# Triple mixers of a two-block kernel: the output product by blocks of columns, with its own buffer for the mix

## The reference

```python
    for l in range(DEPTH):
        x = x + 0.5 * swiglu_2(rms_norm_2(x, ffn1_norm[l]), ffn1_w1[l], ffn1_w3[l], ffn1_w2[l])
        h = rms_norm_2(x, mix_norm[l])
        z = h @ w_in[l]
        ...
        gt = jax.nn.sigmoid(gates.reshape(B, S, N_BRANCH, D))
        mixed = (gt[:, :, 0] * (y_na @ w_br_na[l])
                 + gt[:, :, 1] * (y_gla @ w_br_gla[l])
                 + gt[:, :, 2] * (y_mla @ w_br_mla[l]))
        x = x + mixed @ w_out[l]
        x = x + 0.5 * swiglu_2(rms_norm_2(x, ffn2_norm[l]), ffn2_w1[l], ffn2_w3[l], ffn2_w2[l])
```

## Time and profile before

| | us |
|---|---|
| median of three runs | 2333.51 |
| lowest and highest | 2332.92, 2333.69 |
| the profiled execution | 2333.37 |
| its span | 2331.5 |
| PE busy | 2320.1 |
| DVE busy | 1682.0 |
| ACT busy | 1257.6 |

### The profile page before, as it was taken

One profiled execution on the slowest core, in us unless ns is written; L12 is line 12 of the kernel. 1 busy time (PEld: TensorE's weight loads), 2 busy tenths in 40 slices (PEclk: granted clock), 3 DMA queues, 4 the chain that ended last, 5 costly groups with the idle time before them and its releaser, 6 DMA issues.

```text
span 2331.5 us, 32711 instructions
## 1 busy us (share of the span) xinstructions
PE 2320.1 (100%) x13658; PEld 2026.8 (87%) x13658; DVE 1682.0 (72%) x2148; ACT 1257.6 (54%) x1525; POOL 74.4 (3%) x106
## 2 busy tenths in 40 slices
PE   9999999999999999999999999999999999999999
PEld 8889889888888978888888877888888888788887
DVE  8867846875876789767766766587587667766873
ACT  6545664554554665545545754555455457554552
POOL 2000000000000010100010000001000100000000
PEclk9999999999999999999999999999999999999999
DMA  7655445565655426656655533567565555344664
GB/s 226 196 185 176 145 134 191 183 192 185 196 184 186 153 91 192 207 190 190 195 187 181 176 129 129 167 195 216 185 193 186 184 182 179 118 136 163 192 187 144
DMA packets 335042, 409.51 MB, mean 176 GB/s; under 512 B 7894, under 2 KB 285104, under 8 KB 334896
## 3 DMA queue, kind: packets, MB, share of 16 engines
q1 hardware_dynamic: 331632, 401.66, 53.9%
q0 software_dynamic: 3072, 5.69, 1.0%
q10 hardware_dynamic: 192, 0.08, 0.0%
HBM read 406.35 MB, written 1.05 MB: 175 GB/s over the span
## 4 chain that ended last, share of the span: by engine, by line
PE 93%; DVE 5%; ACT 1%; DMA 1%; issue 0%; SPq 0%; DVEq 0%; ACTq 0%
PE bank L613 13%; PE acc L613 12%; PE bank L1381 11%; PE bank L621 7%; PE acc L621 6%; PE acc L705 6%; PE bank L705 6%; PE acc L692 4%; PE bank L712 3%; PE acc L712 3%; PE acc L789 3%; PE acc L2762 2%; PE acc L1551 2%; DVE part_lo L503 1%; PE bank L651 1%; PE bank L3334 1%
## 5 line engine op out<-in xcount | busy, mean ns | idle before, releaser
L503 DVE TENSOR_TENSOR part_lo<-raw,part_hi 128x2048 fp32r<-128x2048 f32 (+3 forms) x390 | 870.0, 2234 | 345.9 <-ACT part_hi L496 342.7
L496 ACT ACTIVATE part_hi<-raw 128x2048 fp32r<-128x2048 f32 (+3 forms) x390 | 728.4, 1868 | 335.6 <-DMA raw<-in_ffn_w 99.3
L613 PE MATMUL bank<-hT,part_hi 128*128 128x512 f32 x1408 | 328.2, 390 | 0.3 <-ACT part_hi L496 0.3
L613 PEld LDWEIGHTS bank<-hT,part_hi 128*128 128x128 f32 x1408 | 261.7, 188 | 53.2 <-ACT part_hi L496 0.5
L613 PE MATMUL acc<-hT,part_hi 128*128 128x512 f32 x1280 | 298.2, 390 | 0.0
L613 PEld LDWEIGHTS acc<-hT,part_hi 128*128 128x128 f32 x1280 | 237.8, 188 | 47.6
L1381 PE MATMUL bank<-part_hi,hT 128*128 128x512 f32 x768 | 247.4, 395 | 0.7 <-issue 0.7
L621 PE MATMUL bank<-hT,part_lo 128*128 128x256 f32 x1408 | 184.3, 284 | 0.0
L621 PEld LDWEIGHTS bank<-hT,part_lo 128*128 128x128 f32 x1408 | 178.1, 191 | 3.6
L1381 PEld LDWEIGHTS bank<-part_hi,hT 128*128 128x128 f32 x768 | 144.2, 188 | 32.8 <-issue 3.5
L621 PE MATMUL acc<-hT,part_lo 128*128 128x256 f32 x1280 | 166.4, 283 | 0.2 <-DVE part_lo L503 0.2
(11 more groups left out here) (536 smaller groups left out, 3291.5 us busy)
## 6 DMA issues: line engine op xcount, KB each, us to landing
raw<-in_ffn_w SPq DMA_DIRECT2D x122, 1024.0 KB, 5.3
raw<-in_w_in SPq DMA_DIRECT2D x48, 1024.0 KB, 5.1
raw<-in_ffn_w_up SPq DMA_DIRECT2D x44, 1024.0 KB, 5.4
raw<-in_ffn_w_gate SPq DMA_DIRECT2D x43, 1024.0 KB, 5.4
raw<-in_ffn_w_down SPq DMA_DIRECT2D x32, 1024.0 KB, 5.1
raw<-in_hy_w_in SPq DMA_DIRECT2D x22, 1024.0 KB, 5.0
raw<-in_ffn_w_down SPq DMA_DIRECT2D x16, 768.0 KB, 4.3
raw<-in_ffn_w SPq DMA_DIRECT2D x12, 768.0 KB, 4.6
```

What stands on the lines that cost most here:

```text
L496: t.e.activation(part_hi[:, n % SLOTS, 0:size], raw[:, n % SLOTS, 0:size], ACT.Copy).then_inc(hi_ready, 1)
L503: t.e.tensor_tensor(part_lo[:, n % SLOTS, 0:size], raw[:, n % SLOTS, 0:size], part_hi[:, n % SLOTS, 0:size].bitcast(F32), ALU.subtract).th ...
L613: mm = pe.matmul(tiles[:, f, :].rearrange("p (h s) -> p h s", h=2), slot_cols(s, 0)[:, k, f * P:(f + 1) * P], hT[:, :, k, :], start=(first ...
```

## The change

- `mixT` is a buffer of its own for the turned mix, high and low part side by side. Before, the mix lay in `hT`, where the next activations go.
- `w_out` comes as O0: rows 0 to 511 of columns 256 to 767; O1: all rows of columns 0 to 255; O2: rows 512 to 1023 of columns 256 to 767; O3: all rows of columns 768 to 1023. So output tiles 0 and 1 (pair 0) are finished with O1, tiles 2 and 3 in the middle of O2, 4 and 5 with O2, 6 and 7 with O3.
- Each output tile has a whole bank, its low products in the second half: 16 matmuls per piece of 512 columns (`wide`) and 16 of 256 (`narrow`), 128 a layer.
- `mix_out_scalar` and `mix_out_vector` take the place of `down_scalar`, `down_vector`, `pre_scalar` and `pre_vector` here: copy, add, high parts, low parts and squares pair by pair, with the splits of U0 and G1 between them.
- The banks of the turning always start with bank 0.

The diff, without lines of context:

```diff
@@ -332,6 +332,8 @@
+            with ExitStack() as g:
+                mixT = sb("mixT", [P, 2, KD, S], F32R, where=g)
@@ -2716,8 +2719,11 @@
             load_gates(2)
             for r in (0, 2):
                 load_rows(t, A["w_br_mla_2"][l], r)
-            for r in range(0, 8, 2):
-                load_rows(t, A["w_out_2"][l], r)
+            w = A["w_out_2"][l]
+            load(t, cols_of(w, COLS, WIDE)[:, 0:4, :])
+            load_cols(t, w, 0)
+            load(t, cols_of(w, COLS, WIDE)[:, 4:8, :])
+            load_cols(t, w, COLS + WIDE)
 
         def later_loaded(l):
 
@@ -3410,38 +3416,82 @@
-            def out_tile(s, d, k, passes=PASSES):
-                return down_tile(pe, lambda w: slot_rows(s, w)[:, k % 2, :], lambda g: hT[:, g, k, :], d, k == 0,
-                                 k == KD - 1, passes)
+            def out_bank(d):
+                return bank[:, d, :] if d < 2 else acc[:, d - 2, :] if d < 6 else bank[:, d - 4, :]
+            def wide(d, weights, ks, first=False, last=False):
+                for k in ks:
+                    mm = pe.matmul(out_bank(d).rearrange("p (h s) -> p h s", h=2), weights(0, d, k), mixT[:, :, k, :],
+                                   start=(first and k == ks[0]), stop=(last and k == ks[-1]), skip_group_check=True)
+                return mm
+            def narrow(d, weights, ks, first=False, last=False):
+                for k in ks:
+                    mm = pe.matmul(out_bank(d)[:, 0:S], weights(1, d, k), mixT[:, 0, k, :],
+                                   start=(first and k == ks[0]), stop=(last and k == ks[-1]), skip_group_check=True)
+                return mm
+            def half_rows(s, k0):
+                return lambda part, d, k: slot_part(s, part, 4, WIDE)[:, k - k0, (d - 2) * P:(d - 1) * P]
+            def all_rows(s, d0):
+                return lambda part, d, k: slot_cols(s, part)[:, k, (d - d0) * P:(d - d0 + 1) * P]
+            turned = t.banks.next
+            t.banks.skip(-turned % 4)
-            s = arrived(t)
+            w = half_rows(arrived(t), 0)
-            pe.wait_ge(mix_hi, 4 * l + 1)
-            for d in range(4):
-                for k in (0, 1):
-                    out_tile(s, d, k, ((0, 0), (0, 1)))
-            pe.wait_ge(*banks[0])
-            for d in range(4):
-                for k in (0, 1):
-                    out_tile(s, d, k, ((1, 0),))
+            for i in range(2):
+                pe.wait_ge(mix_hi, 4 * l + i + 1)
+                for d in (2, 3):
+                    narrow(d, w, (2 * i, 2 * i + 1), first=(i == 0))
+            for i in range(2):
+                pe.wait_ge(*banks[i])
+                for d in (2, 3):
+                    wide(d, w, (2 * i, 2 * i + 1))
-            for d in range(4, KD):
-                for k in (0, 1):
-                    mm = out_tile(s, d, k)
+            for d in (4, 5):
+                wide(d, w, range(0, 4), first=True)
+            for d in (4, 5):
+                mm = narrow(d, w, range(0, 4))
-            for k0 in range(2, KD, 2):
-                s = arrived(t)
-                for d in range(KD):
-                    for k in (k0, k0 + 1):
-                        if d == 0:
-                            pe.wait_ge(*banks[k // 2])
-                        mm = out_tile(s, d, k)
-                    if k0 == KD - 2 and d in (1, 3, 5):
-                        mm.then_inc(acc_full, 1)
-                mm.then_inc(piece_done, 1)
+            w = all_rows(arrived(t), 0)
+            for d in (0, 1):
+                narrow(d, w, range(0, 4), first=True)
+            for d in (0, 1):
+                wide(d, w, range(0, 4))
+            for i in (2, 3):
+                pe.wait_ge(*banks[i])
+                for d in (0, 1):
+                    wide(d, w, (2 * i, 2 * i + 1))
+            for d in (0, 1):
+                mm = narrow(d, w, range(4, 8), last=True)
+            mm.then_inc(piece_done, 1)
+            w = half_rows(arrived(t), 4)
+            for d in (2, 3):
+                narrow(d, w, range(4, 8))
+            for d in (2, 3):
+                mm = wide(d, w, range(4, 8), last=True)
+            mm.then_inc(mix_pair_full, 1)
+            for d in (4, 5):
+                wide(d, w, range(4, 8))
+            for d in (4, 5):
+                mm = narrow(d, w, range(4, 8), last=True)
+            mm.then_inc(piece_done, 1)
+            w = all_rows(arrived(t), 6)
+            narrow(6, w, range(KD), first=True)
+            wide(6, w, range(KD), last=True).then_inc(first_full, 1)
+            wide(7, w, range(KD), first=True)
+            narrow(7, w, range(KD), last=True).then_inc(piece_done, 1)
+            t.banks.skip(turned)
@@ -3540,12 +3590,102 @@
+            turned = t.banks.next
+            t.banks.skip(-turned % 4)
-                act.activation(hT[:, 0, k0:k0 + 2, :], halves(b), ACT.Copy, scale=0.5).then_inc(mix_hi, 1)
-            down_scalar(t, KD, to_x=True)
+                act.activation(mixT[:, 0, k0:k0 + 2, :], halves(b), ACT.Copy, scale=0.5).then_inc(mix_hi, 1)
+            t.banks.skip(turned)
+            mix_out_scalar(t, l)
+        def mix_out_banks(b):
+            return (bank, acc, acc, bank)[b][:, (0, 0, 2, 2)[b]:(2, 2, 4, 4)[b], :]
+        def mix_out_scalar(t, l):
+            act = t.e
+            at = G_FFN2 + 8 * l
+            def high(k):
+                act.activation(hT[:, 0, k, :], xT[:, k, :], ACT.Copy, scale=gain[:, at + k:at + k + 1]).then_inc(hT_hi, 1)
+            next_hi(t)
+            next_hi(t)
+            for b in range(4):
+                if b < 3:
+                    if b == 0:
+                        act.wait_ge(piece_done, through(t))
+                    elif b == 1:
+                        act.wait_ge(mix_pair_full, l + 1)
+                    else:
+                        act.wait_ge(piece_done, through(t))
+                    act.activation(down_rows[:, :, :], low_of(mix_out_banks(b)), ACT.Copy).then_inc(down_low, 1)
+                    if b != 1:
+                        next_hi(t)
+                else:
+                    act.wait_ge(first_ready, t.see(first_ready))
+                    high(2 * b)
+                act.wait_ge(x_ready, t.see(x_ready))
+                if b < 3:
+                    high(2 * b)
+                high(2 * b + 1)
+                act.activation(square_rows[:, b, :, :], xT[:, 2 * b:2 * b + 2, :], ACT.Square).then_inc(x_squares, 1)
+        def mix_out_vector(t, l):
+            dve = t.e
+            at = G_FFN2 + 8 * l
+            def both_added(f, sig):
+                v = xT[:, 6 + f, :]
+                dve.tensor_tensor(v, low_of(mix_out_banks(3))[:, f, :], v, ALU.add).then_inc(down_added, 1)
+                dve.wait_ge(down_added, t.see(down_added))
+                dve.tensor_tensor(v, high_of(mix_out_banks(3))[:, f, :], v, ALU.add).then_inc(sig, 1)
+                dve.wait_ge(sig, t.see(sig))
+            def low(k):
+                dve.wait_ge(hT_hi, t.see(hT_hi))
+                dve.scalar_tensor_tensor(hT[:, 1, k, :], xT[:, k, :], gain[:, at + k:at + k + 1],
+                                         hT[:, 0, k, :].bitcast(F32), ALU.mult, ALU.subtract).then_inc(hT_ready, 1)
+            next_lo(t)
+            next_lo(t)
+            for b in range(4):
+                if b < 3:
+                    if b == 0:
+                        dve.wait_ge(piece_done, through(t))
+                    elif b == 1:
+                        dve.wait_ge(mix_pair_full, l + 1)
+                    else:
+                        dve.wait_ge(piece_done, through(t))
+                    v = xT[:, 2 * b:2 * b + 2, :]
+                    dve.wait_ge(down_low, t.see(down_low))
+                    dve.tensor_tensor(v, high_of(mix_out_banks(b)), v, ALU.add).then_inc(down_added, 1)
+                    dve.wait_ge(down_added, t.see(down_added))
+                    dve.tensor_tensor(v, down_rows[:, :, :], v, ALU.add).then_inc(x_ready, 1)
+                    dve.wait_ge(x_ready, t.see(x_ready))
+                    if b:
+                        dve.sem_inc(acc_taken, 2)
+                        t.see(acc_taken, 2)
+                    if b != 1:
+                        next_lo(t)
+                    low(2 * b)
+                    low(2 * b + 1)
+                else:
+                    dve.wait_ge(first_full, t.see(first_full))
+                    both_added(0, first_ready)
+                    low(2 * b)
+                    dve.wait_ge(piece_done, through(t))
+                    both_added(1, x_ready)
+                    low(2 * b + 1)
+                dve.wait_ge(x_squares, t.see(x_squares))
+                if b:
+                    t.link(dve.tensor_tensor(square_rows[:, 0, :, :], square_rows[:, 0, :, :], square_rows[:, b, :, :],
+                                             ALU.add))
+            dve.tensor_tensor(sums[:, :], squares[:, 0:S], squares[:, S:2 * S], ALU.add).then_inc(sums_ready, 1)
@@ -3663,15 +3803,18 @@
```

(14 more changed lines are left out.)

## The result

The changed kernel takes 2345.47 us (median of five runs, 2345.16 to 2346.44) against 2333.51 for the kernel before on the same chip: 12.0 us or 0.5% slower, ratio 1.0052 with a 95% interval of 1.004 to 1.0063. The forecast was 2346.

What follows compares the result with a forecast made beforehand. The prediction took PE, busy for 2320.1 of 2331.5 us, to bound the kernel. It summed 2333.37 + 5.5 + 6.0 (handover, layers 1 and 0) + 2 x 0.6 (clock) = 2346 us, range 2339 to 2352.

Steps and rivals of the forecast that it cites:

- The bound: Whole kernel: PE, busy 2320.1 of 2331.5 us, bounds it; time PE loses in the openings stays lost.
- The handover: From product to FFN opening: U0's split delays the pairs' parts, so PE loses 5.5 us in layer 1, 6.0 in layer 0.
- One sign: In the FFN opening: some 7 us of waits of its narrow and wide matmuls per layer, where there was under 1.
- The product: Mixer's output product: 192 matmuls of 256 columns become 64 of 512 and 64 of 256, gaining 0.80 us per layer.
- The clock: In the FFN opening: PE nearly idle, so the clock halves; 0.6 us per layer booked, between nothing and 3.4.
- the nearest row: Sparse mixer: after 9.18 us with PE busy for 6.70, the granted clock was 0.50 for 6.82 us.
- Transfers of w_out: Product's weight pieces in runs of 2 KB and 1 KB instead of 4 KB: nothing to 0.3 us, nothing booked.
- (a): Rival: handover hidden behind O2 and O3, gains arrive, 3.2 us faster, 2330.1; chance 0.06.
- the point of decision: Handover in layer 1: U0 must be split by 2132.5, before pair 0's add is due, for it to be hidden.
- (b): Rival: DVE never waits in the handover from 2138.7, own work 13.8 us; 3.2 and 3.7 us lost, 2340.3; chance 0.12.
- (c): Rival: the half clock in the openings costs its whole price in both layers, 6.8 us, 2351.7; chance 0.12.
- (d): Rival: handover costs what was gained, only pair 3's chain exposed, within 0.2% of before, about 2334; chance 0.06.

Runs made afterwards that it cites:

- the short chain: The changed kernel with U0's and G1's splits moved behind the work and the other handover steps ordered by what PE waits for: 2331.46 us, ratio 0.999 to the kernel before.

## Why the prediction was right

- **The bound** held: what PE left the two openings later, the kernel took longer, 11.8 of the 12.0 us; nothing was won back behind them.
- **The handover** was right in its mechanism and size. PE was to leave the opening 36.03 us (layer 1) and 36.2 us (layer 0) after the first product matmul; it did at 36.18 and 36.31, 0.3 us more in all. U0's load was the first late thing, as laid out: 2131.56 forecast for its issue is 12.2 us after the first product matmul, 12.4 measured. Moving the two splits gave back 5.4 us per layer, and the shares worked out for them were met once the clock was kept up. One sign did not come: some 7 us of waits were to show in each layer, and the rows have 7.5 us in both together. The rest of the longer openings is matmuls at the half level, in place of waits.
- **The product** was mis-sized: 0.80 us per layer forecast, 0.42 measured, and by the prediction's own signs a product that is not 0.8 us shorter counts against it. The step that failed is the pace of 0.2275 us per wide matmul, taken from an FFN run; here it is 0.2335. It hardly moved the time, since the opening's end hangs on the end of O1 and the chain behind it: with `mixT` moved by 32 bytes the product was 0.48 us shorter, and PE left the opening of layer 1 only 0.16 us sooner (36.02 against 36.18). The 2.5 ns per matmul of the Trainium skill (TensorE: Matmul & The Clock Gate, Back-to-back issue gap), which the page gives for an isolated matmul, would have made the gain 0.16; the measured 0.42 lies between the two and nearer to 0.16. The 1.3 us by which the prediction would then have raised the time is too much, since of the product only what lies ahead of the end of O1 moves the chain.
- **The clock** came down in both openings, as the nearest row and the rule on idling of the Trainium skill (TensorE: Matmul & The Clock Gate, Part 1) had it, but the 0.6 us per layer booked for it was not paid: the half level lay on time that was waited out, and with the clock kept the time is the same within 0.2 us.
- **The number** is partly luck. The 1.2 us booked for the clock were not paid; the handover took 0.3 more than forecast, and 0.3 more lie elsewhere in the kernel (2345.47 - 2333.37 = 12.1, of which the two places hold 11.8). What is left is the distance of 0.6 us between 2346.07 and 2345.47.
- **Transfers of w_out** in shorter runs: the view of transfers has 4.9 us for them, as before.
- **The rivals.** (a), hidden handover, is what the short chain does, for 2331.5; in the change U0's split ended 19.6 us after the first product matmul, where 13.2 was the point of decision. But the split did not have to come sooner for it: in the short chain it starts 21.1 us after the first product matmul, later than the 17.7 of the change, and no longer stands ahead of the high parts. (b), less waiting, had DVE's own work right (14.0 us from U0's low part to tile 7's, 13.8 forecast), but DVE waited for ACT's high parts three times on the way, 1.9 us in all. (c), a dearer clock, fell with the run that kept the clock: no difference. (d) needed pairs 0 to 2 in time, and they were not.

## What to carry to other kernels

When work that was done once at a stage's end is cut into parts that overlap the stage, walk each engine's queue and ask of every instruction that stays between two parts what it waits for: a piece of prefetch that was harmless ahead of nothing becomes the head of the chain, and here two such pieces made 10.8 of the 12.0 us lost. With them moved the time was 2334.66 us, about that of the kernel before; the gain of 2.2 us came only when the other steps were ordered too (2331.46). Put prefetch where the engine waits anyway, and the square sums and copies behind what the busiest engine needs next. In the change the half clock was free, because PE waited again behind it; with G1's split moved it cost 2.0 us. So it has to be looked at again after each repair.

## What was unexpected of the hardware

- The pace of matmuls depends on where the moving operand lies: 233.3 ns on average for 512 columns with `mixT` at one place, 229 with it 32 bytes lower, all else the same. The rule is open. FFN runs of 512 columns also begin slower (233, 236, 229, 232, 231 ns) before they settle at 226.7.
- With 40 matmuls of zeros in the longest wait, 2.41 us of work, the granted clock stayed at 1.00 through both openings; without them it was 0.50 for 6.82 us in layer 0 and for 3.41 us in layer 1.
